# Ten points with two slots each on the chain of every tile's branches, and the chain's steps sorted between them

## The reference: what is computed

```
xn = rmsnorm(x);  z = xn @ w_in                      # q, k, v | pooling input | q, k, v, gates of the mLSTM | branch gates
ya = sliding-window attention (128 keys back, 8 heads, 2 kv heads, bias per distance, a sink per head)
yb = (mean over the last 2/4/8/16 tokens - token) @ w_pool
for each chunk of 128 tokens and head (mLSTM):       # carry C, n, m
    b = cumsum(lf);  D = b_l - b_s + ig_s (causal);  m_t = max(b + m, rowmax(D))
    S = (q k^T) * exp(D - m_t);  h = (S v + w_inter * C q) / max(|den|, exp(-m_t))
    C, n, m are carried on with weights exp(...)
x = x + (sum over the branches of sigmoid(gate) * (y @ w_br)) @ w_out
PEER: per token and 8 heads: the top 16 of 16384 experts by product keys
x = x + sum over those 128 experts of gate * gelu(x . u[e]) * v[e]
```

## Time and profile before

| | |
|---|---|
| profiled execution, us | 3825.35 |
| its span, us | 3823.5 |
| granted TensorE clock, mean | 0.931 |
| VectorE busy, us | 2255.4 (59%) |
| ScalarE busy, us | 1102.1 (29%) |
| GpSimd busy, us | 1172.0 (31%) |
| moved in all | 1317.39 MB, mean 345 GB/s |

### The profile page before, as it was taken

The page is one execution under the profiler, slowest core; times in us unless marked ns, Lnnn a source line. Parts: engine busy times, 40 slices in busy tenths (PEclk is TensorE's granted clock), DMA queues, the critical chain, the costliest instruction groups (busy, mean ns, idle before and its releaser), DMA issues. The chain is left out here.

```text
span 3823.5 us, 31573 instructions
## 1 busy us (share of the span) xinstructions
PE 3160.3 (83%) x10006; PEld 1820.0 (48%) x10006; DVE 2255.4 (59%) x5201; ACT 1102.1 (29%) x3314; POOL 1172.0 (31%) x1038
## 2 busy tenths in 40 slices
PE   7798879979989799769979799762699898777777
PEld 4487634546655444436656444431366563222222
DVE  1411777774657767664657688661555487775444
ACT  1210233432223324332223323340221233332222
POOL 0000333333333243333324233230233234443443
PEclk9899989989999899889999899885899999999999
DMA  5134899879999999779999899873899799999998
GB/s 168 60 124 159 348 365 383 349 297 396 420 394 403 365 403 412 303 303 404 420 384 407 349 403 398 324 266 139 331 375 392 278 399 397 421 421 422 421 420 358
DMA packets 204913, 1317.39 MB, mean 345 GB/s; under 512 B 23235, under 2 KB 27387, under 8 KB 72098
## 3 DMA queue, kind: packets, MB, share of 16 engines
q0 software_dynamic: 148608, 1082.20, 69.9%
q1 hardware_dynamic: 52681, 220.59, 15.4%
q10 hardware_dynamic: 3456, 12.58, 0.8%
HBM read 1298.97 MB, written 17.64 MB: 344 GB/s over the span
## 5 line engine op out<-in xcount | busy, mean ns | idle before, releaser
L1857 POOL DMA_INDIRECT arena<-uv,eidx x1032 | 1171.4, 1135 | 2623.2 <-PE ps L889 1889.5
L889 PE MATMUL ps<-arena,dgs 128*128 128x512 f32 x3412 | 1631.1, 622 | 268.4 <-ACT dgs L1189 244.4
L1428 DVE CUSTOM_DVE_ANT_0 arena<-arena,xx 128x1024 f32<-128x1024 f32 x1024 | 1231.8, 1220 | 583.9 <-DMA arena<-uv,eidx 559.5
L889 PEld LDWEIGHTS ps<-arena,dgs 128*128 128x128 f32 x3412 | 652.3, 198 | 1083.1 <-issue 675.0
L1170 ACT ACTIVATE gel<-dots 128x2 f32<-128x2 f32 x516 | 104.4, 202 | 1585.3 <-DVE dots L1428 1584.4
L922 PE MATMUL ps<-wbuf,xT 128*128 128x420 f32 (+1 forms) x1152 | 428.5, 522 | 7.7 <-DMA wbuf<-w_z 6.6
L1069 PE MATMUL ps<-xT,wbuf 128*128 128x256 f32 (+1 forms) x1536 | 356.8, 386 | 5.2 <-DMA wbuf<-w_merge 3.0
L1069 PEld LDWEIGHTS ps<-xT,wbuf 128*128 128x128 f32 x1536 | 295.1, 193 | 74.2 <-issue 19.4
L922 PEld LDWEIGHTS ps<-wbuf,xT 128*128 128x128 f32 (+1 forms) x1152 | 205.2, 181 | 231.1 <-issue 221.7
L1189 ACT ACTIVATE dgs<-cst,wgt 128x128 f32<-128x128 f32 x853 | 305.3, 395 | 16.7
L1662 DVE SCALAR_TENSOR_TENSOR T<-T,ps 128x256 f32<-128x256 f32 (+1 forms) x96 | 40.6, 423 | 434.5 <-PE ps L1073 434.5
(11 more groups left out here) (352 smaller groups left out, 1901.5 us busy)
## 6 DMA issues: line engine op xcount, KB each, us to landing
wbuf<-w_merge SPq DMA_DIRECT2D x96, 768.0 KB, 8.4
wbuf<-w_z SPq DMA_DIRECT2D x64, 840.0 KB, 8.6
wbuf<-w_q SPq DMA_DIRECT2D x64, 512.0 KB, 8.1
arena<-uv,eidx POOLq DMA_INDIRECT x1032, 11.4
wbuf<-w_o SPq DMA_DIRECT2D x32, 512.0 KB, 7.4
xin<-x_prompt SPq DMA_DIRECT2D x8, 1024.0 KB, 8.3
grow<-gains SPq DMA_DIRECT2D x8, 512.0 KB, 9.1
xin<-biasfull SPq DMA_DIRECT2D x4, 1024.0 KB, 4.9
```

The lines of the kernel that those rows point to most:

```text
L889: done = mm(ps[:, half, :], dgs[:, j, :], ring[:, j, row_], start=(q == 0), stop=(q == P - 1), skip_group_check=True)
L1428: v.tensor_tensor_reduce(ring[:, j, 0:D], ring[:, j, 0:D], x, 1.0, 0.0, ALU.mult, ALU.add, dots[:, j:j + 1]).then_inc(s["dotted"], 1)
L1857: g.indirect_dma_start(ring[:, j, :], None, uv, bass.IndirectOffsetOnAxis(ap=experts, axis=0)).then_inc(got[j], 16)
```

## The change

`BRANCH` becomes ten equal weights with the same sum, 24. The points on all three engines are renumbered 0 to 9 and three more are put in, and some steps of the chain move. On TensorE the sum for b comes first, into a free part of bank 3, and its semaphore `cs_mm` is gone (`qk_tr`, which follows, covers it); the pooling goes to bank 7 in place of bank 6, so the wait for its copy (`pooled_ready`) moves from L972 to before L991; before the scores there is a new wait for b's copy. On ScalarE point 0 moves behind the three copies, and points 0, 1, 2 follow one another. On VectorE the copy `qcT` moves behind the diagonal, and the copy of the transposed P (L1633) before the head norm.

```diff
-BRANCH = (4, 4, 2, 2, 4, 2, 6)
+BRANCH = (2.4,) * 10
 # TensorE
                     pe.wait_ge(s["poolT_done"], before)
+                    mm(ps[:, 3, P:P + CH], tri, lf[:, CH * t:CH * t + CH], start=True, stop=True)
...
-                            mm(ps[:, 6, cols_], own, band[:, c, :], start=True, stop=False, skip_group_check=True)
+                            mm(ps[:, 7, cols_], own, band[:, c, :], start=True, stop=False, skip_group_check=True)
...
                     last.then_inc(s["pool_mm"], 1)
-                    mm(ps[:, 7, 0:CH], tri, lf[:, CH * t:CH * t + CH], start=True, stop=True).then_inc(s["cs_mm"], 1)
                     point(p, "b", t, 0)
                     pe.wait_ge(s["diag_ready"], here)
-                    pe.wait_ge(s["pooled_ready"], here)
                     mm(ps[:, 6, :], ones[:, :], tmpi[:, 0:512], start=True, stop=True).then_inc(s["arow_mm"], 1)
...
                     last.then_inc(s["S_mm"], 1)
+                    point(p, "b", t, 1)
                     pe.wait_ge(s["qT_ready"], here)
                     pe.wait_ge(s["kT_ready"], here)
+                    pe.wait_ge(s["tile_v"], tile.at("b_ready", NT * p + t + 1))
...
                     scores(0).then_inc(s["scores_a"], 1)
-
+                    point(p, "b", t, 2)
                     pe.wait_ge(s["M_ready"], here)
+                    pe.wait_ge(s["pooled_ready"], here)
                     mm(ps[:, 7, 0:8], last_row, bM, start=True, stop=True).then_inc(s["bcast_mm"], 1)
-                    point(p, "b", t, 1)
...
                     last.then_inc(s["inter_mm"], 1)
+                    point(p, "b", t, 3)
...
                     scores(1).then_inc(s["scores_mm"], 1)
-                    point(p, "b", t, 2)
+                    point(p, "b", t, 4)
...
                     last.then_inc(s["ST_tr"], 1)
-                    point(p, "b", t, 3)
+                    point(p, "b", t, 5)
...
                     last.then_inc(s["state_mm"], 1)
-                    point(p, "b", t, 4)
+                    point(p, "b", t, 6)
...
                         if half == 0:
-                            point(p, "b", t, 5)
+                            point(p, "b", t, 7)
                             pe.wait_ge(s["PTa_ready"], here)
+                    point(p, "b", t, 8)
                     pe.wait_ge(s["PTd_ready"], here)
...
                     last.then_inc(s["pooly_mm"], 1)
-                    point(p, "b", t, 6)
+                    point(p, "b", t, 9)
 # ScalarE
                     f(kcs, z[:, t, CK0:CK0 + 512], ACT.Copy, scale=float(CD) ** -0.5).then_inc(s["kcs_ready"], 1)
-                    point(p, "b", t, 0)
...
-                    f(pooled, ps[:, 6, :], ACT.Copy).then_inc(s["pooled_ready"], 1)
+                    f(pooled, ps[:, 7, :], ACT.Copy).then_inc(s["pooled_ready"], 1)
+                    point(p, "b", t, 0)
                     point(p, "b", t, 1)
+                    point(p, "b", t, 2)
                     act.wait_ge(s["am_ready"], here)
...
-                    point(p, "b", t, 2)
                     point(p, "b", t, 3)
+                    point(p, "b", t, 4)
                     act.wait_ge(s["L_ready"], here)
...
                     last.then_inc(s["P_exp"], 1)
-                    point(p, "b", t, 4)
+                    point(p, "b", t, 5)
+                    point(p, "b", t, 6)
                     act.wait_ge(s["PTa_tr"], here)
...
-                    point(p, "b", t, 5)
+                    point(p, "b", t, 7)
+                    point(p, "b", t, 8)
                     act.wait_ge(s["PV_mm"], here)
...
-                    point(p, "b", t, 6)
+                    point(p, "b", t, 9)
 # VectorE
-                    dve.wait_ge(s["cq_tr"], here)
-                    dve.wait_ge(s["inter_mm"], before)
-                    v.tensor_copy(qcT, ps[:, 4, :]).then_inc(s["qcT_ready"], 1)
-                    dve.wait_ge(s["cs_mm"], here)
                     dve.wait_ge(s["bcast_mm"], before)
-                    v.tensor_copy(bM[:, 0:CH], ps[:, 7, 0:CH]).then_inc(s["tile_v"], tile.step("b_ready"))
+                    v.tensor_copy(bM[:, 0:CH], ps[:, 3, P:P + CH]).then_inc(s["tile_v"], tile.step("b_ready"))
...
                                     ALU.mult).then_inc(s["diag_ready"], 1)
+                    dve.wait_ge(s["cq_tr"], here)
+                    dve.wait_ge(s["inter_mm"], before)
+                    v.tensor_copy(qcT, ps[:, 4, :]).then_inc(s["qcT_ready"], 1)
                     point(p, "b", t, 1)
...
                     v.tensor_tensor(bM[:, CH:2 * CH], rmax, mprev[:, :], ALU.max).then_inc(s["M_ready"], 1)
+                    point(p, "b", t, 2)
...
                                     rd.unsqueeze(2).broadcast_to([P, CH, CD]), ALU.mult).then_inc(s["tile_v"], tile.step("h_ready"))
+                    point(p, "b", t, 6)
                     normed(1, "P_exp", "aden_ready").then_inc(s["arden_ready"], 1)
...
                     last.then_inc(s["CT_ready"], 1)
-                    point(p, "b", t, 5)
+                    point(p, "b", t, 7)
+                    dve.wait_ge(s["PT_tr"], here)
+                    dve.wait_ge(s["PV_mm"], before)
+                    v.tensor_copy(R[:, 3072:4096], psf[:, 1024:2048]).then_inc(s["PTd_ready"], 1)
+                    point(p, "b", t, 8)
                     dve.wait_ge(s["tile_v"], tile.at("h_ready", NT * p + t + 1))
...
                                     ).then_inc(s["tile_v"], tile.step("hy2"))
-
-                    dve.wait_ge(s["PT_tr"], here)
-                    dve.wait_ge(s["PV_mm"], before)
-                    v.tensor_copy(R[:, 3072:4096], psf[:, 1024:2048]).then_inc(s["PTd_ready"], 1)
-                    point(p, "b", t, 6)
+                    point(p, "b", t, 9)
```

More of the change, by code:

```diff
@@ L139 @@
 interw_ready ST_ready wk_ready nd_ready CT_ready PTd_ready arden_ready poolT_done v_shift
-pooled_ready qk_tr pool_mm cq_tr ck_tr cs_mm arow_mm S_mm scores_a scores_mm bcast_mm inter_mm ST_tr intra_mm
+pooled_ready qk_tr pool_mm cq_tr ck_tr arow_mm S_mm scores_a scores_mm bcast_mm inter_mm ST_tr intra_mm
 state_mm PTa_tr PT_tr PV_mm pooly_mm""".split()
@@ L958, in branches @@
                         if p == t == 0:
-                            mm(ps[:, 6, c * P:c * P + 16], own, first_band[:, c, :], start=True, stop=True)
-                            last = mm(ps[:, 6, c * P + 16:(c + 1) * P], own, band[:, c, 16:P], start=True, stop=True)
+                            mm(ps[:, 7, c * P:c * P + 16], own, first_band[:, c, :], start=True, stop=True)
+                            last = mm(ps[:, 7, c * P + 16:(c + 1) * P], own, band[:, c, 16:P], start=True, stop=True)
                         else:
                             rows_ = z[64:P, 0, PIN0 + c * P:PIN0 + (c + 1) * P] if t else pinprev[64:P, cols_]
-                            mm(ps[:, 6, cols_], own, band[:, c, :], start=True, stop=False, skip_group_check=True)
-                            last = mm(ps[:, 6, c * P:c * P + 16], rows_, prev_band[64:P, c, :], start=False, stop=True, skip_group_check=True)
+                            mm(ps[:, 7, cols_], own, band[:, c, :], start=True, stop=False, skip_group_check=True)
+                            last = mm(ps[:, 7, c * P:c * P + 16], rows_, prev_band[64:P, c, :], start=False, stop=True, skip_group_check=True)
                     last.then_inc(s["pool_mm"], 1)
-                    mm(ps[:, 7, 0:CH], tri, lf[:, CH * t:CH * t + CH], start=True, stop=True).then_inc(s["cs_mm"], 1)
                     point(p, "b", t, 0)
                     pe.wait_ge(s["diag_ready"], here)
-                    pe.wait_ge(s["pooled_ready"], here)
                     mm(ps[:, 6, :], ones[:, :], tmpi[:, 0:512], start=True, stop=True).then_inc(s["arow_mm"], 1)
```

## The result

| | before | after |
|---|---|---|
| median of four runs each, us | 3834.9 (3830.9 to 3838.83) | 3745.58 (3741.42 to 3752.25) |
| ratio, 95% interval | | 0.9769 (0.9748 to 0.979) |
| profiled execution, its span, us | 3825.35, 3823.5 | 3749.68, 3747.9 |

The two profiled executions differ by 75.7 us only: that of before lay 10 us under its median, that of after 4 above. So both kernels were profiled again (before_again, after_again, after_third). The table cuts all five spans at the same instructions; "first" and "second" are the halves of the six tiles with slots, cut exactly at VectorE's hand-over of the maxima (the round stretches of the earlier trace rows gave 248 and 179 for what is 253.6 and 175.4 here), "sample" reaches from the last branch to the first gate product.

The account below looks back on a forecast made before the run. Transfers and TensorE were taken as near their limits outside branches; inside, late rows stalled VectorE in first halves, VectorE bounded second halves. 48.8 - 10 + 6.3 = 45.1 us off the 3836.78 median: 3792 us, range 3763 to 3831.

Parts of the forecast that it names:

- First halves, -48.8: Six first halves of tiles, passes 1 to 3: small points keep gathers running, 248 us falls to 199.2.
- 32 pairs at 1.25: First halves: one remaining wait for rows of 1.25 us charged per pair of slots, added to VectorE's 159.2 us.
- a turn of the ring of 20.1 us in 21.2: First halves: a slot's issue, landing, use and freeing take 20.1 us, just fitting four pairs' 21.2 us.
- Second halves: Six second halves, passes 1 to 3: they give back 10 us, a quarter of a worst case of 40.
- End of a stretch: Last point's slots, left to the merge: six before, two or four after; counted as nothing, 0 to 8 us kept.
- Order, -6.3: Pass 0, two tiles: earlier row product (1.17 us) and PT copy (1.97 us) save 6.3 us, bounds 3 to 9.
- PV in passes 1 to 3: TensorE's wait for the PT copy before PV: put at nothing; 12 us more if VectorE had cover left.
- Rival B: Second halves: late transposes delay VectorE's PT copy, 4.5 us in six tiles; 20.7 us slower, 3857; chance 0.09.
- Rival A: First halves: ring still runs dry each turn, second halves give back all 40; gain only 5 to 25; chance 0.20.
- TensorE's clock: Bursts freeing slots in the branches: 2.6 us lost on one after idling; effects named but left out of the sum.
- the first rule named in the prediction: Idle gaps send TensorE to 1.2 GHz and the next burst pays; fewer such bursts gain up to 10 us (3782).
- A second HAM failure mode: Many short idles may also slow TensorE; pieces stay slow and the ring's turn grows from 20.1 towards 21.2 us.

Follow-up runs that it names:

- before_again: The kernel before, unchanged, run once more for a second profiled execution: 3837.21 us.
- after_again: The changed kernel, unchanged, run a second time: 3747.34 us, ratio 0.9779 to the kernel before.
- after_third: The changed kernel, unchanged, run a third time: 3752.12 us, ratio 0.9779 to the kernel before.
- late_free: The changed kernel without TensorE's points 1 and 2, so TensorE frees their slots at point 3: 3750.80 us, ratio 0.978 to the kernel before.
- six_left: The changed kernel with six slots at the last point of pass 3's second tile and none at its point 1: 3757.18 us, ratio 0.9797 to before.
- pt_late: The changed kernel with VectorE's copy of the transposed P back behind the head norm: 3753.72 us, ratio 0.9807 to the kernel before.
- quiet: The changed kernel without slots in the sample stage's first three points, these placed later: 3752.57 us, ratio 0.9791 to the kernel before.
- stream12: The changed kernel with sample points 2 and 3 before the cache-row waits and 12 slots for 2 at point 2: 3766.73 us, ratio 0.9842 to before.

## Why the prediction was wrong

The direction and the largest term held, and so did the mechanism in the first halves: VectorE's waits for rows fell by more than two thirds once the points were small. Against the spans the forecast missed 35 us of 80; the medians differ by 89 in the first comparison and by 83 and 82 in the two later ones.

1. *First halves, -48.8: right* (-49.2). VectorE idles 203 - 163.34 = 39.7 us there, and 32 pairs at 1.25 had been charged 40. That is partly luck: only 23 us are waits for rows, most of the rest are waits for TensorE. The reason given, a turn of the ring of 20.1 us in 21.2, had the slack too small: late_free frees a pair some 3 us later in each of six halves, which by that slack costs 6 x (3.2 - 1.1) = 13 us, and cost 6.

2. *Second halves: the step that failed.* "They hold 32 pairs too ..., so I take a quarter, 10 us" gave back what was never lost: they became 6.3 us shorter. VectorE bounds them, idling 11 us where it was 14.4, and their rows come in time: cut exactly, its waits for rows there fell from 7.6 us to 0.7, with the same work (161.4 and 161.2 us). A residual wait is to be charged only where the consumer is faster than the stream, and the earlier trace rows showed VectorE busy 164.6 of 179. Against the forecast this step is 16 of the 35 us, the largest part.

3. *End of a stretch: left out for pass 3.* "TensorE leaves the slots of the last point to the merge: six today, two or four after" was followed into the merges (0 to 8 us kept, 5.1 found) and not into the sample stage, where the same slots are gathered beside the cache loads: 11.9 us. six_left shows it.

4. *Order, -6.3: 11.5.* Row product and copy came as forecast (1.16 and 3.18 us earlier), two tiles 6.4; pt_late gives the copy's part as 6.0 against 4 forecast. The rest lies in the second tile's first half (20.4 and 24.5 before, 17.6 and 17.7 after), whose waits I had not read.

5. *PV in passes 1 to 3: nothing, right* (pt_late). Rival B's sign, VectorE over 3 us before its copy for TensorE's transposes, showed in one tile of pass 1 only (3.8 us). Rival A did not come: GpSimd's longest wait in passes 2 and 3 is 5.8 and 8.8 us (15.2 and 17.4 before), 10.6 and 9.3 in after_again; in pass 1, with the fewest slots, it is still 14.7. Searches and projections took 4.1 us back, at the edge of what the executions differ by.

6. *TensorE's clock.* It stands at its full level, 1.00, in four of six first halves; before, all six lay at 0.84 to 0.95. In after_again one of them fell to 0.86 and took 36.7 us in place of 32.0, with TensorE busy 35.17:
```profile
1589.76:1626.43 36.67, 35.17 (x114) 20.26 (x115) 26.33 (x48) 13.73 (x34) 14.22 (x14) 0.86 0.82 329
```
That half's first piece of twelve instructions took 7.87 us, against 5.4 at the same place in after. So the first rule named in the prediction (the Trainium skill, TensorE: Matmul & The Clock Gate, "HAM oscillation") agrees with this trace, and the second ("A second HAM failure mode") does not: with more and shorter pieces the clock stood higher. The forecast kept the clock out of its sum; what part of the 49.2 us it is, no run separates.

## What to carry to other kernels

Where a stream is worked off between the steps of a chain, make the pieces small before sorting the steps: pieces of two in place of four gave two thirds of the gain in the branches, less by rows that came in time than by chain steps that no longer stood behind a long piece. When slots move, follow the last of them into whatever stage begins there. And don't read a transfer wait with a low DMA share as room before you know on how many engines the transfer runs: two loads split at 112 partitions gave 46 us, over half of what the whole change gave.

## What the runs showed of the hardware

A load of 127 partitions moved 20 GB/s at a share of 0.08 with nothing beside it (after, 2556 to 2572 us), and SP's queue stood 29.3 us in the issue behind it. With gathers beside such a load that issue took 36.6 to 79.3 us, 2.4 to 3.1 us more for each, at mean shares of 0.43 (quiet) to 0.75 (stream12). Issued as 112 and 15 partitions, the same bytes held SP for 2.2 us in the row that had taken 41.8, and for 7.2 us at most in its stage.
